# Decoder block on one core: expert tokens gathered for two expert pairs at once, and the last row of gains loaded late

## The reference

```
h  = rmsnorm(x) * (1 + sc2) + sh2
lg = h @ w_group + b_group          # top 1 of 4 groups
le = h @ w_router + b_router        # top 2 of 8 experts in that group
cw = weight of each token for each of the 32 experts (0 where not chosen)
for each expert e:                  # w_gate, w_up: 2048 x 512, w_down: 512 x 2048
    hid = silu(h @ w_gate[e]) * (h @ w_up[e])
    y  += (hid * cw[:, e]) @ w_down[e]
out = x + gt2 * rmsnorm(y, g_post_ffn)
```

## Time and profile before

| | |
|---|---|
| median of three runs | 1563.5 us |
| the profiled execution | 1562.75 us |
| its span | 1560.4 us |
| first expert begins (line 1163) | 623.8 us into the span |
| last w_down matmuls (line 1109) end, last scatter (line 1125) begins | 1541 us |
| PE busy | 1511.8 us (97%) |
| bytes moved | 589.96 MB, mean 378 GB/s |

### The profile page before, as it was taken

One profiled execution on the slowest core, in us unless ns is written; L12 is line 12 of the kernel. 1 busy time (PEld: TensorE's weight loads), 2 busy tenths in 40 slices (PEclk: granted clock), 3 DMA queues, 4 the chain that ended last, 5 costly groups with the idle time before them and its releaser, 6 DMA issues.

```text
span 1560.4 us, 19229 instructions
## 1 busy us (share of the span) xinstructions
PE 1511.8 (97%) x7984; PEld 811.9 (52%) x7984; DVE 681.7 (44%) x1228; ACT 231.8 (15%) x443; POOL 41.2 (3%) x57
## 2 busy tenths in 40 slices
PE   4999999999999999999999999999999999999996
PEld 2888888855654446344344344344444434434432
DVE  3565757676877635232232232232232332322325
ACT  2100311111232303011011011011011010010003
POOL 2000000000001200000000000000000000000003
PEclk9999999999999999999999999999999999999999
DMA  9999567699878996899999999999999999999994
GB/s 360 398 385 374 208 259 300 251 361 365 307 301 293 365 411 248 357 428 428 428 428 428 429 429 428 428 428 430 404 429 429 427 428 430 430 428 427 429 429 179
DMA packets 102323, 589.96 MB, mean 378 GB/s; under 512 B 5745, under 2 KB 16465, under 8 KB 76929
## 3 DMA queue, kind: packets, MB, share of 16 engines
q1 hardware_dynamic: 99904, 580.93, 91.7%
q0 software_dynamic: 1696, 5.66, 1.0%
q10 hardware_dynamic: 672, 2.66, 0.5%
HBM read 587.07 MB, written 2.16 MB: 378 GB/s over the span
## 4 chain that ended last, share of the span: by engine, by line
PE 71%; DMA 22%; SPq 3%; DVE 3%; issue 0%; ACTq 0%; ACT 0%; DVEq 0%
PE bank L1163 21%; DMA ring<-in_w_up 20%; PE bank L1196 8%; PE bank L923 7%; PE bank L673 5%; PE bank L639 5%; PE bank L1077 4%; PE bank L864 4%; PE bank L1057 3%; SPq L380 2%; DMA ring<-in_w_ada 2%; PE bank L707 2%; PE bank L686 1%; PE bank L689 1%; DMA ring<-in_w_in 1%; PE bank L1088 1%
## 5 line engine op out<-in xcount | busy, mean ns | idle before, releaser
L1163 PE MATMUL bank<-ring,RN 128*64 128x512 f32 x1488 | 330.6, 593 | 7.9 <-DMA ring<-in_w_up 7.9
L1163 PEld LDWEIGHTS bank<-ring,RN 128*64 128x64 f32 x1488 | 106.7, 137 | 220.7 <-issue 200.2
L1196 PE MATMUL bank<-ring,RN 128*64 128x512 f32 x992 | 219.7, 595 | 0.5 <-issue 0.5
L2212 DVE TENSOR_TENSOR RN<-bank,RN 64x512 f32<-64x512 f32 x31 | 21.5, 693 | 374.0 <-ACT RN L1517 374.0
L1196 PEld LDWEIGHTS bank<-ring,RN 128*64 128x64 f32 x992 | 68.9, 137 | 137.4 <-issue 135.6
L2219 DVE COPY RG<-bank 64x512 f32<-64x512 f32 x64 | 44.1, 689 | 196.1 <-PE bank L1196 188.4
L1057 PEld LDWEIGHTS bank<-RN,RX 128*128 128x128 f32 x976 | 111.5, 192 | 13.0 <-issue 13.0
L1057 PE MATMUL bank<-RN,RX 128*128 128x128 f32 x976 | 115.7, 277 | 0.0
L923 PE MATMUL bank<-ring,RT 128*128 128x512 f32 x256 | 113.0, 596 | 0.8 <-DVE RT L1999 0.8
L1163 PE MATMUL bank<-RT,RN 128*64 128x512 f32 x256 | 112.3, 592 | 0.0
L1077 PE MATMUL bank<-RG,RN 128*128 128x512 f32 x240 | 109.5, 599 | 0.0
(11 more groups left out here) (395 smaller groups left out, 1474.8 us busy)
## 6 DMA issues: line engine op xcount, KB each, us to landing
ring<-in_w_down SPq DMA_DIRECT2D x64, 2048.0 KB, 15.4
ring<-in_w_up SPq DMA_DIRECT2D x48, 2048.0 KB, 20.2
ring<-in_w_gate SPq DMA_DIRECT2D x47, 2048.0 KB, 16.0
ring<-in_w_ada SPq DMA_DIRECT2D x32, 2048.0 KB, 10.4
ring<-in_w_in SPq DMA_DIRECT2D x18, 2048.0 KB, 9.2
RT<-in_w_gate SPq DMA_DIRECT2D x17, 2048.0 KB, 15.5
RH<-in_w_up SPq DMA_DIRECT2D x16, 2048.0 KB, 20.0
ring<-in_w_ada SPq DMA_DIRECT2D x18, 1024.0 KB, 18.5
```

The costliest lines, as they stand in the source:

```text
L1163: last = mm(bank[0][64 * s:64 * s + 64, :], tokT[:, k, q * CAP:(q + 1) * CAP], w[:, k % 8, :], start=k == 0, stop=k == KT - 1, skip_group_ ...
L1196: last = mm(bank[2 + n % 2][64 * (n // 2):64 * (n // 2) + 64, :], hidT[:, k * CAP:(k + 1) * CAP], wdn[:, n * BLK:(n + 1) * BLK], start=k = ...
```

## The change

From pair 2 on, tokens are gathered for two pairs at once. DVE writes `onehot4`, 256 slots wide, for four experts. `gather_two_pairs` makes them in eight parts of four matmuls with 256 columns, in the second expert of pairs 1, 3, 5, ... 13 (seven times); the second expert of pairs 2, 4, ... 14 gathers none. DVE writes the first pair of a part to `tokT` and the second to a new buffer `tok_odd`, which is `RG[:, 1, :]`, the place of the last row of gains. So the row of gains is now loaded when the last expert's gate and up matmuls are done. Parts 0 to 2 stand behind the gate and up matmuls, part 3 behind the transposes, and parts 4 to 7 one behind each of the four k steps of w_down. Pair 1's tokens are gathered in pair 0 as before. The order of SP's issues is the same.

```diff
+            def gather_two_pairs(n, ms):
+                for m in ms:
+                    if m == 0:
+                        pe.wait_ge(sig("gathered_used").sem, (n - 1) * 4)
+                    if m >= 3:
+                        pe.wait_ge(sig("gathered_used").sem, (n - 1) * 4 + (m - 2))
+                    for k in (2 * m, 2 * m + 1):
+                        for tt in range(TT):
+                            last = mm(bank[GB[m % 3]][:, (k % 2) * S:(k % 2 + 1) * S], x_t[:, tt, k * P:(k + 1) * P],
+                                      onehot4[:, tt, :], start=tt == 0, stop=tt == TT - 1)
+                    last.then_inc(sig("gathered").sem, 1)
...
-                    if q == 1:
+                    if q == 1 and not scatter_last:
                         pe.wait_ge(sig("onehot").sem, p + 2)
                         for m in range(3):
                             gather_part(p + 2, m)
+                    if q == 1 and four is not None:
+                        pe.wait_ge(sig("onehot").sem, four + 2)
+                        gather_two_pairs(p + 2, range(3))
...
-                    if q == 1:
+                    if q == 1 and not scatter_last:
                         gather_part(p + 2, 3)
+                    if q == 1 and four is not None:
+                        gather_two_pairs(p + 2, (3,))
...
                         if k % 2 == 1:
                             last.then_inc(sig("expert_used").sem, 1)
+                        if q == 1 and four is not None:
+                            gather_two_pairs(p + 2, (4 + k,))
 
             pair(0, True, False)
-            with pe.Fori(1, NE // 2 - 1) as p:
-                pair(p, True)
-            pair(NE // 2 - 1, False)
+            pair(1, True, four=1)
+            with pe.Fori(1, NE // 4 - 1) as g:
+                pair(g * 2, True, two="used")
+                pair(g * 2 + 1, True, odd=True, two="", four=g + 1)
+            pair(NE // 2 - 2, True, two="used")
+            pair(NE // 2 - 1, False, odd=True, two="")
...
-            wait(pool, "gate2_out", 16)
+            pool.wait_ge(sig("expert_used").sem, (NE - 1) * HB + 4)
             pool.dma_start(RG[:, 1, :], late_rows[3 * KT:4 * KT, :].rearrange("(o k) p -> o (k p)", o=1).to_broadcast([P, D]))\
                 .then_inc(sig("gain2_in").sem, 16)
...
+            def onehot_two_pairs(n, g):
+                dve.wait_ge(sig("gathered").sem, (n - 1) * 4)
+                for tt in range(TT):
+                    for q in range(4):
+                        e = g * 4 + q
+                        last = ts(onehot4[:, tt, q * CAP:(q + 1) * CAP], iota, rank[:, tt, bass.ds(e, 1)], sel_rstd[:, tt, bass.ds(e, 1)],
+                                  ALU.is_equal, ALU.mult)
+                last.then_inc(sig("onehot").sem, 1)
+
+            def tokens_two_pairs(n):
+                for m in range(8):
+                    dve.wait_ge(sig("gathered").sem, (n - 1) * 4 + (m + 1))
+                    for k in (2 * m, 2 * m + 1):
+                        for b, dst in enumerate((tokT, tok_odd)):
+                            c0 = (k % 2) * S + b * P
+                            ins = ts(dst[:, k, :], bank[GB[m % 3]][:, c0:c0 + P], aff[:, 2, k:k + 1], aff[:, 3, k:k + 1], ALU.mult, ALU.add)
+                    ins.then_inc(sig("gathered_used").sem, 1)
```

More of the change, by code:

```diff
@@ L290, in block_kernel @@
         onehot = RN[:, 2048:2304].rearrange("p (t s) -> p t s", t=TT)
+        onehot4 = RN[:, 4096:4608].rearrange("p (t s) -> p t s", t=TT)
+        tok_odd = RG[:, 1, :].rearrange("p (k s) -> p k s", k=KT)
         hid = RN[:, 2304:2816]
@@ L1087, in last_expert @@
                         c = 64 * (k % 2)
-                        last = mm(bank[4 * (n % 2)][c:c + 64, :], tokT[:, k, CAP:2 * CAP], w[:, k % 8, :],
+                        last = mm(bank[4 * (n % 2)][c:c + 64, :], tok_odd[:, k, CAP:2 * CAP], w[:, k % 8, :],
                                   start=k < 2, stop=k >= KT - 2, skip_group_check=True)
@@ L1126, in last_scatter, with pair @@
                        start=True, stop=True).then_inc(sig("scattered").sem, 1)
-            def pair(p, gather_next, scatter_last=True):
+            def pair(p, gather_next, scatter_last=True, odd=False, two=None, four=None):
+                tok = tok_odd if odd else tokT
                 for q in range(2):
@@ L1137, in pair @@
                     for k in range(KT):
-                        if q == 0 and k % 4 == 0:
+                        if q == 0 and two is None and k % 4 == 0:
                             pe.wait_ge(sig("gathered_used").sem, p * 4 + (k // 4 + 1))
+                        if q == 0 and two == "used" and k % 2 == 0:
+                            pe.wait_ge(sig("gathered_used").sem, p * 4 + (k // 2 + 1))
                         if k == 4 and first:
@@ L1162, in pair @@
                             w = AHEAD if ahead and n == 2 else ODD[n] if q == 1 and n < 2 else ring[:, n, :, :]
-                            last = mm(bank[0][64 * s:64 * s + 64, :], tokT[:, k, q * CAP:(q + 1) * CAP],
+                            last = mm(bank[0][64 * s:64 * s + 64, :], tok[:, k, q * CAP:(q + 1) * CAP],
                                       w[:, k % 8, :], start=k == 0, stop=k == KT - 1, skip_group_check=True)
@@ L2186, in add_scattered, with pair @@
                     ins.then_inc(sig("scatter_added").sem, 1)
-            def pair(p, gather_next, scatter_last=True, first=False):
+            def pair(p, gather_next, scatter_last=True, first=False, four=None):
                 for q in range(2):
@@ L2192, in pair @@
                         weighted_onehot(p + 1)
-                    if q == 1 and gather_next:
+                    if q == 1 and not scatter_last:
                         onehot_pair(p + 2)
+                    if q == 1 and four is not None:
+                        onehot_two_pairs(p + 2, four)
                     if q == 1 and not gather_next:
@@ L2214, in pair @@
                         add_scattered(p, first)
-                    if q == 1 and gather_next:
+                    if q == 1 and not scatter_last:
                         tokens(p + 2)
+                    if q == 1 and four is not None:
+                        tokens_two_pairs(p + 2)
                     dve.wait_ge(sig("expert_used").sem, e * HB + 6)
@@ L2228, in _ @@
             pair(0, True, False)
-            pair(1, True, first=True)
-            with dve.Fori(2, NE // 2 - 1) as p:
-                pair(p, True)
+            wait(dve, "gate2_out", 16)
+            pair(1, True, first=True, four=1)
+            with dve.Fori(1, NE // 4 - 1) as g:
+                pair(g * 2, True)
+                pair(g * 2 + 1, True, four=g + 1)
+            pair(NE // 2 - 2, True)
             pair(NE // 2 - 1, False)
```

## The result

The changed kernel is slower: 1582.74 us median of four runs (1579.27 to 1584.5) against 1562.78 us for the kernel before; the ratio is 1.0122, 95% interval 1.011 to 1.0134, which is 17 to 21 us. The forecast was 1573.0 us, range 1568 to 1580. The direction and the mechanism were right, the size was half of what came, and the time lies outside the range. The nearest case is the first rival, "more places run dry" (1579.4 us by its sum), which had 15%.

The account below looks back on a forecast made before the run. The prediction took the queue of weight loads to set the end, losing time when it runs empty. Holes of 4.05 us (expert 3) and 5.8 us (expert 15), taken as 9.5 us, on 1563.5 gave 1573.0 us, range 1568 to 1580.

Parts of the forecast that it names:

- the first rival: Rival at 15%: a double-gather expert 2 us longer than taken also empties the queue at experts 7 and 11; 16 us, 1579.4 us.
- What bounds the kernel: Over the experts: the queue of loads sets the end, 29.4 us an expert against 28.54 us for PE on average.
- Length of the double-gather expert: The expert where two pairs are gathered: 6.9 us longer than now, 6.5 of gather plus 0.4 for entries into w_down.
- the price of the entries into w_down: In the double-gather expert, w_down is entered four times instead of once: 0.4 us taken, bounds nothing and 2 us.
- The sum: Whole kernel: holes of 4.05 and 5.8 us make 9.85, or 8.95 with the windows' 0.9 us; 9.5 us taken.
- Expert 3: First double gather: expert 4 begins 6.9 us later, the queue holds 2.85 us, so it is empty for 4.05 us.
- The count of 23 pieces: Before expert 4's issue at 742.85 us: SP has issued 23 pieces from 632.99 us, giving the queue work until 747.0 us.
- Experts 7 and 11: Double gathers there: next issue takes effect at L + 37.0 against queue end L + 38.1; nothing lost, by 1.1 us.
- Expert 15: Before the change of issue order at expert 16: queue empty from L + 38.1 to L + 43.9, 5.8 us.
- the second hole: At the issue-order change, in front of w_down's piece issued at 1110.30 us: the existing 1.44 us loss stays.
- The clock: Rival at 3%: PE's open waits in seven experts drop the clock to 1.2 GHz; over 20 us, 1590 us.
- The gains: Row of gains loaded near the end, needed 11.2 us after issue: 0 us taken, bounds 0 and 1.

## Why the prediction came out as it did

*What bounds the kernel*: right in the main. Up to expert 15 PE waits for loads and is 9.64 us late (1072.33 against 1062.69), all by the queue. Behind it, the double gather made PE's four experts 117 us long, not 115.4, as slow as the loads, so that both gave the same end. Half of the gather's work taken away left 3.3 us of loss, not a gain.

*Length of the double-gather expert*: the step that failed. It was too short by 1.0 us (6.9 forecast, 7.9 measured), and the term is the price of the entries into w_down, taken as 0.4 us in all from one entry of 0.16. In truth each of the four parts and four groups inside pays, 0.19 and 0.11 us, which is 1.2 us, and 0.15 us more falls at the head of the next expert. Each 1 us of length is lost in up to four holes. The run with w_down in one piece has the forecast length (35.66 us), and there the count of the holes came nearly true: 3.9, 0.5, 0.3 and 5.9 us more than before, where 4.05, 0, 0 and 5.8 were forecast. Even so it was 14 to 15 us slower than the kernel before by its runs, 12.6 by its span; small losses as in *The sum* below make up most of the rest.

*Expert 3*: 4.05 us forecast, 5.2 measured: 7.9 - 2.85 = 5.05. The count of 23 pieces was right; only the length was off. The loss stands in two places, not one: about 1.3 us around 743, before the last piece of w_down, issued at 742.13 us, and the rest from 748 to 753 us.

*Experts 7 and 11*: nothing lost was forecast, by 1.1 us, and dips there were named as a sign of being wrong. They came, with 1.8 and 2.1 us. The length alone used up the room: with L, as in the forecast, for the landing that the expert waits for in the middle of its gate and up matmuls, SP's issue came at L + 37.1 in both (870.59 and 990.83, with L at 833.45 and 953.69), 1.4 us later than the forecast's L + 35.7. The rest is the end of the queue, set to L + 38.1 by data that end 1.1 us before a landing, from the shortest landing of the earlier trace rows. Windows of 1 us show it run dry earlier (a full window is 428):

```profile
870.00:871.00 1.00, 1.00 (x8) 0.40 (x6) 0.00 (x0) 0.00 (x0) 0.00 (x0) 1.00 0.35 148
...
990.00:991.00 1.00, 1.00 (x6) 0.29 (x4) 0.00 (x0) 0.00 (x0) 0.00 (x0) 1.00 0.08 33
...
1110.00:1111.00 1.00, 1.00 (x8) 0.34 (x6) 0.00 (x0) 0.00 (x0) 0.00 (x0) 1.00 0.12 49
```

That is about L + 36.9 at expert 7, L + 36.3 at expert 11 and L + 37.7 at expert 15 (L = 1072.29). My own rows had the warning. By the forecast's formula there was no hole in front of piece 2 of expert 17 in the kernel before (37.0 against 38.1), and the windows show 0.9 us; there too the queue ran dry at about L + 36.9 (L = 1062.65):

```profile
1099.00:1100.00 1.00, 1.00 (x4) 0.49 (x3) 0.17 (x1) 0.59 (x1) 0.00 (x0) 1.00 0.50 213
```

I had instead used the 0.9 us as a correction to subtract. The extra work in expert 11 alone shows the same (1.6 us where 0.2 was counted).

*Expert 15*: 5.8 us forecast, 7.55 us measured in the two windows from 1110 us, or 6.6 more than the 0.9 of before; the second hole stayed at 1.44, as forecast. SP's issue came at 1116.29, L + 44.0, where the forecast has L + 42.6: 1.4 us by the length again, and 0.4 us by the end of the queue.

*The clock*: counted at 3% as a case of over 20 us. In the traced execution it fell in one short expert, after 1.6 us of idle time, less than the 1.96 us that had left it at 1.00, and cost 1.7 us of PE's time. It is a term of at most a few us, not a case.

*The gains*: right, nothing. The load took 8.1 us of the 10.8 between its issue and DVE's first add.

*The sum*: 4.05 + 0 + 0 + 5.8 was 9.85; measured 5.2 + 1.8 + 2.1 + 6.6 = 15.7, against 18.05 in the tail. Of the 2.3 us between, 2.0 are small losses in four windows (780, 900, 1020 and 1480 us, 0.4 to 0.6 us each) that the forecast did not have; what makes them is open. The forecast's sum was short by 1.1 us at expert 3, 1.8 and 2.1 at experts 7 and 11, 0.8 at expert 15 and these 2.0. The first rival had the same four places, but for an expert 2 us longer than forecast; it was 1 us longer, and the queue's earlier end and the small losses came on top.

## What to carry to other kernels

Where a queue of loads sets the pace, ask of each edit when it releases places, not how much work it saves: gathering work of two stages into one makes the mean better and the longest gap between releases worse, and the queue pays for the gap. Count what the queue holds at its lowest point, place by place, and calibrate the count on a hole that the trace already has; a count that says "no hole" where the trace shows one is off by at least that hole there, and probably elsewhere too. Put a price on each change from one kind of work to another inside a stretch, both ways, and multiply its error by the number of places in which it is lost. A margin as wide as its own error is not a margin, and the case beyond it belongs in the range.

## What the runs showed of the hardware

- A landing under load doesn't tell when a piece's data end. The shortest was 7.3 us for 2 MB, which splits as 1.3 us to start, 4.9 of transfer and 1.1 of completion. But with eight pieces of 4.90 us queued behind a landing, the queue ran dry 36.3 to 37.7 us behind it, so the data ended 1.5 to 2.9 us before the landing that PE waited for. That is worked out from where the rate fell, not seen.
- Float32 matmuls of 256 columns took 0.48 us each in groups of four between groups of another shape, and 0.43 to 0.45 in rows of four to sixteen that stand together.
- The clock fell after short idle times: in the changed kernel after 1.08 and 0.52 us close together (0.67 in that window of 5 us), while the other short experts, with the same open waits, stayed at 1.00, and in the kernel before 1.96 us in a window left it too. Executions of the changed kernel differ in it (0.988 to 0.994), and by 3 to 5 us with it. Executions also differ in a fall at 73 to 80 us, by up to 1.6 us in sixteen matmuls.
- 1 MB of gains, one row of memory read into 128 partitions, landed in 11.7 us beside other loads, and in 8.1 and 6.5 us at the end of the weights.
